# First mixer of a fused two-block layer: 36 of its 64 weight products on operands split into two rounded parts, and one chunk of the routed units moved behind a turn

## The reference

```python
# first block
proj = x @ w_in                                # 1024 x 10240: da_q da_k da_v r_q r_k r_v r_g m_q gate0..2
y_da  = diff_attention(da_q, da_k, da_v, ...)  # 8 heads
y_ret = silu(r_g) * retention(r_q, r_k, r_v, ...)   # 4 heads
m_k, m_v = split(mem @ w_mem_kv)
y_mem = memory_attention(m_q, m_k, m_v)        # 4 heads
merged = sum_n sigmoid(gate_n + b_gate) * (branch_n @ w_branch[n])
x = layer_norm(ALPHA * x + merged @ w_o)
x = layer_norm(ALPHA * x + hier_moe(x))        # 4 groups of 4 experts, top 2
# second block
mod = silu(c) @ ada_w[l] + ada_b[l]            # two layers, 6 x 1024 each
# l=0: pooling + windowed attention, then a SwiGLU of width 2816
# l=1: spatial gating, then 8 experts of width 3584, top 2
```

## Time and profile before

| | |
|---|---|
| median of 3 runs | 2287.96 us (2287.62 to 2293.89) |
| the profiled execution | 2286.17 us, its span 2284.1 us |
| first mixer, first routed part | 0 to about 544 us, to about 840 us |
| TensorE busy | 2199.2 us (96%) |
| VectorE, ScalarE busy | 1605.4 us (70%), 1268.4 us (56%) |
| mean granted TensorE clock | 0.981 of full speed |
| HBM read | 641.60 MB |

### The profile page before, as it was taken

The page is one execution under the profiler, slowest core; times in us unless marked ns, Lnnn a source line. Parts: engine busy times, 40 slices in busy tenths (PEclk is TensorE's granted clock), DMA queues, the critical chain, the costliest instruction groups (busy, mean ns, idle before and its releaser), DMA issues.

```text
span 2284.1 us, 25008 instructions
## 1 busy us (share of the span) xinstructions
PE 2199.2 (96%) x10024; PEld 1799.8 (79%) x10024; DVE 1605.4 (70%) x1943; ACT 1268.4 (56%) x1528; POOL 17.7 (1%) x16
## 2 busy tenths in 40 slices
PE   8999999999999979899989899999999999999997
PEld 7658877888888866778858788888888888888885
DVE  0266244547999963445422799999999999999997
ACT  1145113105777753334420677778877787878784
POOL 0000000000000000000000000000000000000000
PEclk9999999998999989999999799999999999999999
DMA  9466455666999972045450699999999999999994
GB/s 361 190 249 238 149 220 221 250 266 260 385 369 349 350 295 111 8 177 221 165 203 1 265 401 347 384 360 367 359 371 371 355 377 341 377 354 384 342 375 156
DMA packets 54063, 646.49 MB, mean 283 GB/s; under 512 B 5808, under 2 KB 11824, under 8 KB 15024
## 3 DMA queue, kind: packets, MB, share of 16 engines
q1 hardware_dynamic: 49232, 630.34, 71.4%
q10 hardware_dynamic: 3264, 9.18, 1.1%
q0 software_dynamic: 1440, 5.24, 0.6%
HBM read 641.60 MB, written 3.15 MB: 282 GB/s over the span
## 4 chain that ended last, share of the span: by engine, by line
PE 93%; DVE 3%; ACT 2%; DMA 1%; issue 1%; DVEq 0%; SPq 0%; ACTq 0%
PE psum L1852 60%; PE psum L1642 19%; PE psum L1632 5%; PE psum L1966 2%; PE psum L1585 1%; PE psum L1874 1%; DMA ring<-w_branch_in 1%; PE psum L1862 1%; DVE arena L606 1%; DVE h_lo L1532 0%; PE psum L1751 0%; PE psum L1664 0%; ACT h_hi L1067 0%; PE psum L1651 0%; ACT mixer_tiles L812 0%
## 5 line engine op out<-in xcount | busy, mean ns | idle before, releaser
L1425 DVE TENSOR_TENSOR stage_lo<-ring,stage_hi 128x1024 fp32r<-128x1024 f32 (+1 forms) x934 | 1104.4, 1216 | 89.2 <-ACT stage_hi L1015 72.2
L1015 ACT ACTIVATE stage_hi<-ring 128x1024 fp32r<-128x1024 f32 (+1 forms) x934 | 963.6, 1055 | 297.3 <-PE psum L1852 225.7
L1852 PE MATMUL psum<-stage_hi,x_hi 128*128 128x512 f32 (+1 forms) x1344 | 530.3, 395 | 3.3 <-DVE arena L1521 2.6
L1852 PE MATMUL psum<-stage_hi,x_lo 128*128 128x512 f32 (+1 forms) x1344 | 521.8, 388 | 0.0
L1852 PE MATMUL psum<-stage_lo,x_hi 128*128 128x512 f32 (+1 forms) x1344 | 520.4, 387 | 0.0
L1852 PEld LDWEIGHTS psum<-stage_hi,x_lo 128*128 128x128 f32 x1344 | 252.9, 188 | 53.4
L1852 PEld LDWEIGHTS psum<-stage_hi,x_hi 128*128 128x128 f32 x1344 | 253.2, 188 | 53.0 <-issue 4.4
L1852 PEld LDWEIGHTS psum<-stage_lo,x_hi 128*128 128x128 f32 x1344 | 253.4, 189 | 49.2
L1852 PE MATMUL psum<-stage_hi,h_hi 128*128 128x512 f32 x664 | 260.1, 392 | 9.8 <-DVE h_lo L1532 9.8
L1852 PE MATMUL psum<-stage_lo,h_hi 128*128 128x512 f32 x664 | 258.6, 389 | 0.0
L1642 PE MATMUL psum<-arena,ring 128*128 128x256 f32 x1024 | 227.4, 382 | 9.0 <-DMA arena<-x_in 8.2
(11 more groups left out here) (219 smaller groups left out, 1609.8 us busy)
## 6 DMA issues: line engine op xcount, KB each, us to landing
ring<-moe_w_gate_in SPq DMA_DIRECT2D x56, 2048.0 KB, 9.3
ring<-moe_w_up_in SPq DMA_DIRECT2D x56, 2048.0 KB, 9.6
ring<-moe_w_down_in SPq DMA_DIRECT2D x56, 2048.0 KB, 9.2
ring<-w_in SPq DMA_DIRECT2D x48, 2048.0 KB, 9.5
ring<-ada_w_in SPq DMA_DIRECT2D x15, 2048.0 KB, 8.0
ring<-w_in_in SPq DMA_DIRECT2D x13, 2048.0 KB, 10.6
mixer_tiles<-ada_w_in SPq DMA_DIRECT2D x9, 2048.0 KB, 7.7
mixer_tiles<-w_in_in SPq DMA_DIRECT2D x6, 2048.0 KB, 12.2
```

The costliest lines, as they stand in the source:

```text
L1015: act.activation(chunk_view(stage_hi, f, side, p, c), chunk_source(f, side, p, c), ACT.Copy)\
L1425: dve.tensor_tensor(chunk_view(stage_lo, f, side, p, c), chunk_source(f, side, p, c), chunk_view(stage_hi, f, side, p, c).bitcast(F32), AL ...
L1852: ins = pe.matmul(dst, a, b, start=start, stop=stop)
```

## The change

1. Nine of the products of the first mixer (`SPLIT`) are made of three fp32r products each: 28 steps with the weights stationary, and 8 steps of `da_v` and `m_v` in four pairs (`TURNED`), a pair being 48 matmuls of 128 x 512. A new step `stage` rounds a chunk of 128 x 1024 of the panel on ScalarE into one of four buffers (`HIS`) and subtracts on VectorE, in place in the slot; 2 chunks for a step, 4 for a pair of `TURNED`. `with_stages` puts it ahead of the step before the one that uses it. A new step `split` does the same with a quarter (128 x 512) of the other operand: x, x again after `m_q`, mem, yret, ymem, merged.
2. The list of steps is written anew: `lam` and two `ada` steps stand between `da_v` and the first head, `branch0` is among the retention heads, `gate1`, `m_k` and `m_v` come ahead of the memory heads, and `gate2` and `branch1` are among those.
3. x is loaded a second time ahead of `w_o`, since its split has overwritten it.
4. In the routed units the last `D` chunk of the last panel but one is put behind the last `turn`; `h_hi` and `h_lo` of even and odd panels lie in different halves.

```diff
+SPLIT = ("da_k", "da_v", "gate1", "m_k", "m_v", "branch1", "gate2", "branch2", "w_o")
+TURNED = ("da_v", "m_v")
+def with_stages(steps):
+    jobs = [n for n, q in enumerate(steps) if q[0] == "gemm" and not (q[1] in TURNED and q[2] % 2)]
+    at = {}
+    for before, n in zip(jobs, jobs[1:]):
+        if steps[n][1] not in SPLIT:
+            continue
+        where = before
+        while steps[where - 1][0] in ("ret_score", "mem_score") and steps[before][1] not in TURNED:
+            where -= 1
+        at.setdefault(where, []).append(("stage",) + steps[n][1:])
 def mixer1_steps():
...
+    s = gemms("da_q", 0) + splits("x", 0, 1, 2, 3) + gemms("da_q", 1, 2, 3) + gemms("da_k", 0, 1, 2, 3)
+    s += gemms("da_v", 0, 1, 2, 3) + [("lam", 0, 0)] + ada(0, 1)
     for h in range(DA_H):
         s += [("da_score", h, 0), ("da_score", h, 1), fill.pop(0)]
         if h:
             s += [("da_norm", h - 1, 0)]
+        s += [fill.pop(0), ("da_turn", h, 0)] + ada(2 + h) + [("da_out", h, 0)]
     s += [("ret_score", 0, 0), ("da_norm", DA_H - 1, 0)]
+    fill = gemms("m_q", 0, 1, 2, 3) + gemms("branch0", 0, 1, 2, 3)
     for h in range(RET_H):
+        s += [("ret_out", h, 0)] + (splits("x_late", 0, 1, 2, 3) if h == RET_H - 1 else [])
+        s += [fill.pop(0)] + ada(10 + h) + [("ret_mean", h, 0)]
+        s += ([("ret_score", h + 1, 0)] if h + 1 < RET_H else []) + [fill.pop(0), ("ret_var", h, 0)]
+    s += gemms("gate1", 0, 1) + splits("mem", 0, 1, 2, 3) + gemms("gate1", 2, 3) + ada(14)
+    s += gemms("m_k", 0, 1) + ada(15) + gemms("m_k", 2, 3) + ada(16)
+    s += gemms("m_v", 0, 1) + ada(17) + gemms("m_v", 2, 3) + splits("yret", 0, 1, 2, 3) + ada(18)
+    s += [("mem_score", 0, 0)] + gemms("branch1", 0)
+    for h in range(1, MEM_H):
+        s += [("mem_score", h, 0)] + gemms("gate2", h - 1) + [("mem_turn", h - 1, 0)] + gemms("branch1", h)
+        s += [("mem_out", h - 1, 0)] + ada(18 + h)
+    s += splits("ymem", 0, 1, 2) + [("mem_turn", MEM_H - 1, 0)] + gemms("gate2", 3) + [("mem_out", MEM_H - 1, 0)]
+    s += splits("ymem", 3)
+    for i in range(4):
+        s += gemms("branch2", i) + splits("merged", i) + (ada(22 + i) if i < 2 else [])
     s += [("gemm", "w_o", i) for i in range(3)]
...
+            d = chunk("D", p)
+            n_d = len(d) - 1 if routed and p == last - 1 else len(d)
+            s += g[:n] + [("turn", p)] + g[n:] + chunk("U", p + 1) + d[:n_d]
...
-        s += [("turn", last)]
+        s += [("turn", last)] + d[n_d:]
...
@@ ScalarE's walk
+                if kind == "stage":
+                    for n, c in staged_chunks(s):
...
+                        if n >= HIS:
+                            act.wait_ge(*chunk_use[n - HIS])
+                        act.activation(staged_hi(s, n), staged_source(s, c, False), ACT.Copy).then_inc(w_hi_set, 1)
...
@@ VectorE's walk
+                if kind == "stage":
+                    for n, c in staged_chunks(s):
+                        dve.wait_ge(w_hi_set, n + 1)
+                        dve.tensor_tensor(staged_source(s, c, True), staged_source(s, c, False),
+                                          staged_hi(s, n).bitcast(F32), ALU.subtract).then_inc(w_lo_set, 1)
+                elif kind == "split":
+                    dve.wait_ge(in_hi_set, split_at[(a, i)])
+                    dve.tensor_tensor(lo, from_, hi.bitcast(F32), ALU.subtract).then_inc(in_lo_set, 1)
...
@@ TensorE, split_product
+            for m, (n, c) in enumerate(staged_chunks(s)):
+                pe.wait_ge(w_lo_set, n + 1)
+                hi, lo = staged_hi(s, n), staged_source(s, c, True)
+                for k in range(KT):
+                    if i == 0 and m == 0 and k % 2 == 0:
+                        pe.wait_ge(in_lo_set, split_at[(SPLIT_OF[a], k // 2)])
+                    for j, (wt, xt) in enumerate(((hi, x_hi), (hi, x_lo), (lo, x_hi))):
+                        ins = pe.matmul(bank(b, 2, T)[:, m, :], wt[:, k, :], xt[:, k, :], start=(k + j == 0),
+                                        stop=(k == KT - 1 and j == 2))
```

More of the change, by code:

```diff
@@ L110, in shape_constants @@
     return out
+SPLIT = ("da_k", "da_v", "gate1", "m_k", "m_v", "branch1", "gate2", "branch2", "w_o")
+TURNED = ("da_v", "m_v")
+SPLIT_OF = {"da_k": "x", "da_v": "x", "gate1": "x_late", "gate2": "x_late", "m_k": "mem", "m_v": "mem",
+            "branch1": "yret", "branch2": "ymem", "w_o": "merged"}
+def with_stages(steps):
[8 more added lines that the diff above has]
+        at.setdefault(where, []).append(("stage",) + steps[n][1:])
+    out = []
+    for n, q in enumerate(steps):
+        out += at.get(n, []) + [q]
+    return out
 def norm_steps(a, last=()):
@@ L121, in mixer1_steps, with gemms, splits, ada @@
 def mixer1_steps():
[L123 to L126, removed]
+    def gemms(name, *jobs):
+        return [("gemm", name, i) for i in jobs]
+    def splits(name, *parts):
+        return [("split", name, i) for i in parts]
+    def ada(*panels):
+        return [("ada", 0, n) for n in panels]
+    s = gemms("da_q", 0) + splits("x", 0, 1, 2, 3) + gemms("da_q", 1, 2, 3) + gemms("da_k", 0, 1, 2, 3)
+    s += gemms("da_v", 0, 1, 2, 3) + [("lam", 0, 0)] + ada(0, 1)
+    fill = [q for name, n in (("r_q", 2), ("r_k", 2), ("r_v", 4), ("r_g", 4), ("gate0", 4)) for q in gemms(name, *range(n))]
     for h in range(DA_H):
@@ L459, in build @@
         for s in plan:
-            if s[0] in ("ada", "lam"):
+            if s[0] in ("ada", "stage", "split", "lam"):
                 continue
@@ L1594, in walk @@
                 kind, a, i = s
[L1595 removed]
+                if s in staged:
+                    split_product(s)
+                elif kind == "gemm" and a in TURNED:
+                    pass
+                elif kind == "gemm":
                     at, fills = panel_of(s)
@@ L1607, in walk @@
                                 evacuated(("da_out", n, 0))
-                        elif a == "branch1":
-                            pe.wait_ge(ret_y, RET_H)
-                        elif a == "branch2":
-                            for n in range(MEM_H):
-                                evacuated(("mem_out", n, 0))
-                        elif a == "w_o":
-                            pe.wait_ge(merged_set, 1)
                         elif a == "ev_o":
```

199 lines of the change are left out of this document (142 added, 57 removed).

## The result

| | before | changed |
|---|---|---|
| median | 2290.93 us (4 runs, 2287.62 to 2294.41) | 2264.98 us (4 runs, 2263.92 to 2267.12) |
| profiled execution, its span | 2286.17, 2284.1 | 2267.12, 2265.3 |
| TensorE clock | 0.981 | 0.976 |
| first mixer ends (first product of the routed part) | 543.62 | 527.82 |

The ratio is 0.9894, with an interval of 0.9879 to 0.9908: faster by 1.1%, 26 us. The prediction was 2262 in a range of 2243 to 2277, a sum of -26.1.

What follows compares the result with a forecast made beforehand. TensorE was taken to bound the kernel almost throughout. Products -43.6, routed units -8.3, waits that go -3.5, new waits +25.6 and clock +3.7 sum to -26.1 on the profiled 2286.2: 2260.1, as median 2262 us, range 2243 to 2277.

Steps and rivals of the forecast that it cites:

- Products: First mixer: 28 split steps at 5.76 instead of 6.91 us, 4 pairs at 10.88 instead of 13.74; 43.6 us less.
- Rival D: Split products in the first mixer: weight loads set the pace, 0.188 us each instead of 0.12; slower, 2324 us; chance 0.03.
- (a): First head: `lam` and two `ada` steps hold VectorE, so TensorE waits 4.7 us.
- (b): `gate1` 0 and 1: staging stands behind other work on VectorE and ScalarE, wait 2.75 us; `ret_out` 0 adds 0.3.
- (c): Memory heads: TensorE waits for staging and copies at `branch1`, `mem_out`, `branch1` 0 and `gate2` 0; 6.4 us.
- (d): `branch2` 0: staging stands behind `ada` 21 and three splits; wait 3.05 us.
- (e): `branch2` 2, `branch2` 3 and first `w_o` step: VectorE needs 9.8 us per step against TensorE's 5.76; 8.4 us.
- Rival B: First mixer: VectorE is ahead, so the waits (a) to (e) are covered; 2233 us, or 2247 with half; chance 0.17.
- rival C: First mixer: VectorE is later than walked, (c) to (e) grow by about 10 us; 2272 us; chance 0.12.
- The clock: TensorE at half clock behind long waits: (a) and (d) in full, 0.5 at the end of (e); 3.7 us more.
- Routed units: Twelve routed units lose their TensorE waits for `h_lo`, as products now lie between; 8.3 us less.
- At nothing: First mixer: panel loads and the second load of x are issued over 20 us ahead and cost nothing.

Runs made afterwards that it cites:

- mixer's part alone: Changed kernel without the routed move (the D chunk stays ahead of the last turn): 2275.97 us, ratio 0.9931 to the kernel before.
- routed move alone: Kernel before with only part 4 of the change (last D chunk behind the last turn, halves of h by panel): 2278.72 us, ratio 0.9948.
- two buffers: Changed kernel with two buffers for rounded chunks instead of four: 2282.07 us, ratio 0.9960 to the kernel before.
- `ada` late: Changed kernel with `ada` 21 behind the staging of `branch2` 1, and 22 and 23 behind `w_o` 0 and 2: 2257.93 us.

## Why the prediction was right, step by step

**Products: right.** 28 steps and 4 pairs were to save 43.6. Steps take 5.70 to 5.71 instead of 6.91, pairs 11.0 and 11.2 instead of 13.7: 44.2. Rival D is out: products that each load other weights, with the weights stationary, run 0.12 us apart (22.81 / 192), though a load's record is 195 ns on average on the page:

```profile
L1766 PE MATMUL psum<-mixer_split 128*128 128x256 f32 x640 | 112.3, 289 | 11.7 <-DVE mixer_split L1366 7.0
L1766 PEld LDWEIGHTS psum<-mixer_split 128*128 128x128 f32 x640 | 95.3, 195 | 13.7 <-issue 12.7
```

The Trainium skill's rule (TensorE: Matmul & The Clock Gate, Part 3, The mechanism) that loads overlap only where row groups differ doesn't describe this: all these use the whole array of 128*128. The same section also lets a load go ahead if it targets the background weight buffer; that would agree with the trace, which doesn't show where a load goes.

**New waits: right in place, 4.9 us too large.**

| | predicted | printed |
|---|---|---|
| (a) first `da_turn` | 4.7 | 4.82 |
| (b) `gate1` 0 and 1, `ret_out` 0 | 3.05 | 2.63 |
| (c) memory heads | 6.4 | 4.37 |
| (d) `branch2` 0 | 3.05 | 2.40 |
| (e) `branch2` 2, 3, `w_o` 0 | 8.4 | 6.46 |

Walking the three orders by hand with row durations found every place, and (a) to 0.1 us. In (e) the wait of `branch2` 3 was to be 4.5 and is 2.67: the step ahead of it took 7.4 instead of 5.7. VectorE's chain to that wait (`ada` 23, then the staging) doesn't depend on that step, so its 1.7 us came out of the wait: 2.67 and 1.7 are 4.4. What was really too large is then (c), by 2.0. Rival B is out, since the waits are there, and rival C too: (c) to (e) came out smaller than walked and not larger.

**The clock: wrong in size.** I charged 3.7. It cost 2.4 in (a) and 1.7 at each of `branch2` 0, 2 and 3, where I had 1.6 at the first two places and 0.5 for the rest: 7.5. Two steps of the prediction failed. One is "eight products, 1.6 us", taken from the earlier trace rows as the length of such a spell. The other is "VectorE decides and TensorE's slowness hides" in (e): it held for `branch2` 2, whose 1.7 came out of the next wait, but not for `branch2` 3, since VectorE needs that step's result before it can split the last quarter of `merged`. Another 2.3 is in the norm behind `w_o`, which I had at nothing: from the transposes ahead of the last step of `w_o` to the mixer's end it is 28.4 us instead of 27.25 less 1.2. The kernel before shows this too, in its second trace (29.65), so it can't be put down to the change. Together 9.8.

**Mixer's length.** Products -44.2, waits that went -3.5 and -0.8 (a late panel), new ones +20.7, clock +9.8, x landing later +0.9: -17.1. It is 15.8 shorter; I had said 18, ending at 526, and it was 527.8. The 1.3 that are left may be what print leaves out of 14 waits; that is not shown.

**Routed units: too small.** 8.3 predicted, 10.0 by the second and fourth stretches (mixer's part alone against the changed kernel), 12.1 in the other pair (before against routed move alone), 11.0 and 11.7 by medians. The mechanism is the one named; the size was read from printed waits instead of from distances of starts.

**At nothing.** Panels and the second load of x: no transfer but the first x releases a wait in the mixer. Right.

**What I had no term for.** In nine of twelve traces the stretch from the second mixer to the second routed part takes 429.4 to 430.4 us, in both traces of the kernel before and in the one with two buffers 424.9 to 425.6. No instruction differs there between the changed kernel and the one with two buffers, or between the kernel before and its routed move alone. So neither part of the change makes it by itself; the 5 us go with the clock, which in the nine is at its lower level for some 10 us at the last heads. What decides is open. The three traces without that long spell are those in which the second mixer starts latest (855.9 to 858.5 us, the others 812 to 852), which may or may not be the reason; nothing was tried on it. It bears on why the first two spans differ by 18.8 and the medians by 26: the span of the kernel before is one without those 5 us, and without the 2.4 of the norm. Its runs reach from 2285.85 to 2297.38, but what clock the untraced ones had isn't known.

So the sum came out within 3 us partly by luck, because errors cancelled: 2 to 4 us on the routed move and 5 on the waits in the kernel's favour, 6 on the clock in the first mixer and 5 in the second against it. The profiled execution, for which the sum was worked out as 2260.1, took 2267.12, which is 7 more.

**Table loads.** The prediction took 1.28 without a drain. The waits of `mem_out` came out at 0.78 and 0.77, not 2.8 longer, and ScalarE goes on at once in the changed kernel:

```profile
85.07 1.28 ACT L953 ACT_TABLE_LOAD   x1
86.37 0.20 ACT L953 ACTIVATE arena<-arena 128x2 f32<-128x2 f32 x1
```

The drain of 1.38 that the Trainium skill counts (ScalarE: Activation LUTs, What ACT_TABLE_LOAD costs) isn't there.

## What to carry to other kernels

When staging for a faster product goes to engines that are half idle, share of busy time says nothing; walk their order and look for the long operation that needn't stand there. Two steps put ahead, three put off and a filler in seven gaps of 0.8 us brought the gain from 26 us to 54 (2238.11 us, the best version here). Price a wait by the distance of starts against an unblocked place, not by its printed length, and give the slow spell of TensorE behind each long wait a term of its own. Trace the unchanged kernel twice before you put a few microseconds down to the change: its norm behind `w_o` alone differed by 2.4 us between two traces.

## What the runs showed of the hardware

- A wait of TensorE cost some 0.25 us more than the trace prints in both places where it was measured (2.01 against 0.36 us between starts where 1.41 is printed; 17.82 against 16.81 where 0.74 is).
- Behind waits of 4.8, 2.4, 3.1 and 2.7 us of TensorE in the changed kernel, and of 2.0 with `ada` late, the granted clock was at its lower level; behind those of 1.3 and 1.6 us it wasn't (the 336 products from 315.86 on take 0.12 us each). The length of the wait alone doesn't decide: behind one of 2.34 us the kernel before kept 1.00 in its first trace (918.28), and the changed kernel, with the same wait, had 0.69.
- The same instructions, with the same waits to 0.1 us, ran at 1.00 in one trace and at 0.69 in another; it cost some 5 us in nine of twelve. At the norm behind `w_o` the two traces of one program had 0.73 and 0.59, and 2.4 us between them.
- VectorE stood idle for 5.7 to 6.0 us between the last routed unit of the first part and the norm; the chain names no releaser ("issue"), in each of three traces looked at (842.53, 837.34 and 823.68 us). The wait printed for TensorE ahead of that norm is 5.95 in the kernel before, 5.8 with the routed move alone, 8.5 with the mixer's part alone and 8.3 in the changed kernel, so it isn't the routed move that lengthens it. By distance of starts, from VectorE's `y_split` to the second mixer's first product, the four take 19.4, 18.9, 20.0 and 20.1 us: some 0.7 is lost there and not 2.4.
